# Latent attention on one core: a pair's value products moved into one group in the next even head, its totals moved ahead of the odd head's turn

## The chip, the cores and the metric

The kernel runs on one core of one Trainium2 chip, in one launch. The metric is the device time of that core in microseconds (us); lower is better. All four compute engines take part: TensorE (PE: matmuls, and PEld for the loads of their weights), VectorE (DVE), ScalarE (ACT) and GpSimd (POOL). SyncE (SP) only issues DMAs.

## The reference

Two transformer blocks over 512 tokens of width 1024 are computed one after the other: retention plus sparse attention and a convolution feed-forward, then an mLSTM and gating mixer, two feed-forwards and, between those, the latent attention that the change touches. Cut to that part:

```python
def mla_mixer(h, positions, w_in, q_g, kv_g, w_uq, w_ukv, w_out):
    ...
    qf = jnp.concatenate([q[..., :C_NOPE], q_rope], axis=-1)
    kf = jnp.concatenate([kv[..., :C_NOPE],
                          jnp.broadcast_to(k_rope, (bsz, seq, C_HEADS, C_ROPE))], axis=-1)
    v = kv[..., C_NOPE:]
    scale = (C_NOPE + C_ROPE) ** -0.5
    ...
        s = jnp.einsum("bqhd,bkhd->bhqk", qblk, kf, preferred_element_type=jnp.float32) * scale
        pr = jax.nn.softmax(s, axis=-1)
        return jnp.einsum("bhqk,bkhd->bqhd", pr.astype(v.dtype), v)
    ...
    return o @ w_out
```

There are 16 heads of 64 + 32 query and key columns and 64 value columns, and no mask: every query sees all 512 keys.

## The kernel before, in words

Every engine runs its own list of instructions in the order in which the Python code calls them, and waits on semaphores (`wait_ge`). There is no scheduler: the order on PE is the order of the loop at L1625 to L1656.

The stage works head by head, `n` from 0 to 15, and two heads make a pair, `p = n // 2`. Keys go by four tiles of 128 (`kt`), queries stay 512 wide. Scores and projections split each number into a high and a low part and take three matmuls each (`product`, L771 to L773). For a head PE does:

- `maxima(n)` (L1135): four matmuls of the high parts, from which DVE takes the negated row maxima (`largest_of`, L3088, into `mla_negm`). They are issued one head ahead, into banks 2 and 3 by turns, and wait for DVE to have read their bank (`mx_done`).
- `turn(n)` (L1140): a transpose of the maxima, which DVE spreads into the queries (`shift_of`, L3093, signal `shift_ready`). It waits for all four maxima of head n. `scores(n, 0)` waits for `shift_ready`.
- `scores(n, kt)` (L771 to L773): key by query scores in PSUM bank 4 or 5. ACT takes the exponential (`weights_of`, L1966) into the tile `c_raw` for an even head, `ev` for an odd one. Those tiles are overwritten two heads later, for which ACT waits for the value products (`pv_done`) and for the sums that POOL makes of them (`add_weights`, L733, `weights_added`).
- `values(p, kt)` (L1165): the weights of both heads of pair p times the values of one quarter of the keys, into bank 6 or 7; four calls, each of four matmuls in full float32, which the trace records as eight.
- `totals(p)` (L1178): ones times the POOL sums of both heads, into bank 1. DVE makes reciprocals of them (`shares`, L3100 to L3102), multiplies (`pair_result`, L3109), and ACT and POOL split the result (L1970, L740).
- Projections for coming pairs: `project_nope` and `project_quad` into bank 0, and `project_k` into bank 1.

Bank 1 is thus shared. `project_k(p + 1)`, in even head 2p, leaves the next pair's keys there; ACT takes the high part (L2356) and DVE the low part (`k_lower`, two instructions at L3632, signal `k_low`). `totals(p - 1)`, in odd head 2p + 1, may only overwrite bank 1 when both are done, and says so in L1173: `pe.wait_ge(k_low, min(2 * p + 6, HEADS))`. It waits besides for `weights_added` of its pair and for the earlier totals to be taken.

In an odd head DVE's own order is: the last two maxima of the next head, `k_lower` twice, `shift_of`, the low part of a weight panel (L2433), in every second odd head `quad_take`, then `shares(p - 1)` and `pair_result(p - 1)`.

On PE an odd head n = 2p + 1 ends with `scores(n, 2)`, `turn(n + 1)`, `values(p, 0)`, `values(p, 1)`, `totals(p - 1)`, `scores(n, 3)`, and in heads 1, 5 and 9 a `project_quad`. The even head behind it has `scores(n, 0)`, two maxima, `values(p - 1, 2)`, `values(p - 1, 3)`, `scores(n, 1)`, `project_nope`, two maxima, and so on.

Of the kernel before, what the change touches and what calls it, by code (L numbers as in the profile page):

```python
# [23 lines left out]
NT = S // P  # L24
# [30 lines left out]
PAIRS = HEADS // 2  # L55
# [123 lines left out]
def build_in(nc, A, ctx):  # L179
# [197 lines left out]
    def cols_of(half):  # L377
        return slice(256 * half, 256 * half + 256)
# [68 lines left out]
    def pair_bank(p):  # L447
        return 6 + p % 2

    def weights_tile(n, kt):  # L450
        return (c_raw if n % 2 == 0 else ev)[:, kt, :]

    def weights_sum(n):
        return tmp[:, n % 4, :]
# [313 lines left out]
    def _(pe):  # L768
# [324 lines left out]
        def project_nope(p):  # L1093
            pe.wait_ge(w_lo_ready, pair_panel(p) + 1)
            if p:
                pe.wait_ge(quad_taken, p // 2 + 1)
            if p >= 2:
                pe.wait_ge(nope_low, 2 * p)
            for k in range(3):
                last = product(ps[:, nope_bank(p), :], w(pair_panel(p), k * P, (k + 1) * P), (cq_hi[:, k, :], cq_lo[:, k, :]),  # L1100
                               k == 0, k == 2)
            last.then_inc(nope_done(p)[0], 1)

        def project_k(p, between=None):
            pe.wait_ge(w_lo_ready, pair_panel(p) + 1)
            if p:
                pe.wait_ge(k_low, 2 * p)
            if p >= 3:
                pe.wait_ge(totals_taken, p - 2)
            for k in range(2):  # L1110
                a = 384 + k * P
                if k and between is not None:
                    between()
                last = product(ps[:, 1, :], w(pair_panel(p), a, a + P), (cq_hi[:, 3 + k, :], cq_lo[:, 3 + k, :]), k == 0, k == 1)
            last.then_inc(k_done(p)[0], 1)

        def project_quad(i):
            pe.wait_ge(w_lo_ready, pair_panel(2 * i) + 1)
            if i:
                pe.wait_ge(nope_low, 4 * i)  # L1120
            for k in range(3):
                a = 640 + k * P
                last = product(ps[:, 0, :], w(pair_panel(2 * i), a, a + P), (cq_hi[:, k, :], cq_lo[:, k, :]), k == 0, k == 2)
            last.then_inc(quad_proj, 1)

        def maxima(n, tiles=range(NT)):
            p, slot = n // 2, n % 4
            if tiles.start == 0:
                pe.wait_ge(nope_high, n + 1)
                pe.wait_ge(k_high, n + 1)  # L1130
                pe.wait_ge(rope_placed, 4 * p + 1 + n % 2)
            for t in tiles:
                if 4 * n + t >= 2:
                    pe.wait_ge(mx_done, 4 * n + t - 1)
                nc.tensor.matmul(ps[:, 2 + t % 2, :], q_hi[:, slot, t * P:(t + 1) * P], k_hi[:, slot, :], start=True,  # L1135
                                 stop=True).then_inc(mx_ready, 1)

        def turn(n):
            pe.wait_ge(mx_done, 4 * n + 4)
            nc.tensor.transpose(ps[0:4, 2, 0:P], mla_negm[:, n % 2, :], ident).then_inc(negm_turned, 1)  # L1140

        def scores(n, kt):
            p, slot, m = n // 2, n % 4, 4 * n + kt
            if kt == 0:
                pe.wait_ge(nope_low, n + 1)
                pe.wait_ge(k_low, n + 1)
                pe.wait_ge(rope_placed, 4 * p + 3 + n % 2)
                pe.wait_ge(shift_ready, n + 1)
            if m >= 2:
                pe.wait_ge(exp_done, m - 1)  # L1150
            else:
                pe.wait_ge(v_copied, 7 + m)
            at = slice(kt * P, (kt + 1) * P)
            product(ps[:, 4 + m % 2, :], (k_hi[:, slot, at], k_lo[:, slot, at]), (q_hi[:, slot, :], q_lo[:, slot, :]),
                    True, True).then_inc(s_ready, 1)

        def values(p, kt):

            pe.wait_ge(exp_done, 4 * (2 * p + 1) + kt + 1)
            if kt == 0 and p >= 2:  # L1160
                pe.wait_ge(pair_out, p - 1)
            for half in range(2):
                for a in range(2):
                    n = 2 * p + a
                    last = nc.tensor.matmul(ps[64 * a:64 * a + 64, pair_bank(p), cols_of(half)], mla_v[:, kt, n, :],  # L1165
                                            weights_tile(n, kt)[:, cols_of(half)], start=kt == 0 and half == 0, stop=kt == NT - 1,
                                            skip_group_check=True)
            last.then_inc(pv_done, 1)

        def totals(p):  # L1170

            pe.wait_ge(weights_added, 6 * p + 6)
            pe.wait_ge(k_low, min(2 * p + 6, HEADS))  # L1173
            if p:
                pe.wait_ge(totals_taken, p)
            for half in range(2):
                for a in range(2):
                    last = nc.tensor.matmul(ps[64 * a:64 * a + 64, 1, cols_of(half)], ones[:, 0:64],  # L1178
                                            weights_sum(2 * p + a)[:, cols_of(half)], start=half == 0, stop=True, skip_group_check=True)
            last.then_inc(totals_out, 1)  # L1180
# [444 lines left out]
        for n in range(HEADS):  # L1625
            p, more, even = n // 2, n + 1 < HEADS, n % 2 == 0
            scores(n, 0)
            if more:
                maxima(n + 1, range(0, 2))
            if even and p:  # L1630
                values(p - 1, 2)
                values(p - 1, 3)
            scores(n, 1)
            if even and p + 1 < PAIRS:
                project_nope(p + 1)
            if more:
                maxima(n + 1, range(2, 4))
            scores(n, 2)
            if even:
                if p + 1 < PAIRS:  # L1640
                    project_k(p + 1, between=lambda: turn(n + 1))
                else:
                    turn(n + 1)
                scores(n, 3)
            else:
                if more:
                    turn(n + 1)
                values(p, 0)
                values(p, 1)
                if p:  # L1650
                    totals(p - 1)
                scores(n, 3)
                if n % 4 == 1 and p + 2 < PAIRS:
                    project_quad(p // 2 + 1)
        values(PAIRS - 1, 2)
        values(PAIRS - 1, 3)  # L1656

        def out_part(panel, ks):

# [2278 lines left out]
```

## Time and profile before

| what | us |
|---|---|
| runs of the kernel | 1861.06, 1862.37, 2248.74 |
| their median | 1862.37 |
| the profiled execution, its own time | 1861.49 |
| its span, first to last instruction | 1859.6 |
| PE busy | 1819.3 |
| the stage of latent attention that the change touches, about | 1318 to 1462 of the span |

The rows of the timeline give the start from the span's beginning, the duration, the engine and the line, what is written and read, how often, and in brackets how long the engine was idle before and what released it. Matmuls are pipelined, so durations of neighbours overlap: what a matmul costs is the step from its start to the next start. A place in the stage is found by the turn (L1140), of which there is one a head: the turns of heads 2, 4, 6, 8, 10, 12 and 14, which PE issues in heads 1, 3, 5, 7, 9, 11 and 13, begin at 1334.59, 1353.12, 1370.13, 1389.50, 1406.49, 1425.88 and 1442.88.

### The profile page before, as it was taken

What the parts mean: (1) busy time and instruction counts of PE and PEld (TensorE: products, weight loads), DVE (VectorE), ACT (ScalarE), POOL (GpSimd) and SP (SyncE); (2) the same over time, 40 slices, a digit from 0 to 9 for tenths busy, and PEclk for the clock granted to TensorE, in tenths of its full rate; (3) what the DMA queues carried; (4) which work ended last, traced back from release to release, by engine and by line L of the source; (5) the groups of instructions that cost most, each with busy time, mean ns of one, the idle gap of its engine ahead of it and who ended that gap; (6) DMA issues with size and microseconds to landing.
All of it is one profiled execution on the core that took longest, in us unless ns stands there. A gap on an engine that the chain in (4) does not pass through costs nothing.

```text
span 1859.6 us, 26472 instructions
## 1 busy us (share of the span) xinstructions
PE 1819.3 (98%) x9682; PEld 1505.2 (81%) x9682; DVE 1320.1 (71%) x1805; ACT 814.9 (44%) x1219; POOL 419.6 (23%) x356
## 2 busy tenths in 40 slices
PE   8999999999999999999999999999999999999998
PEld 6787558888888888887888998988666688989897
DVE  7867876784764778777686766786787567758584
ACT  6365334442432444555453434444444344425252
POOL 0021452100000021010034150502477212514230
PEclk9999999999999999999999999999999999999999
DMA  5242013222232332311323232322101123223232
GB/s 217 91 136 69 1 69 102 79 91 101 91 102 91 102 113 80 102 57 46 99 98 104 93 111 92 107 98 79 57 24 34 46 91 102 99 96 112 91 103 91
DMA packets 48239, 166.00 MB, mean 89 GB/s; under 512 B 5376, under 2 KB 7424, under 8 KB 48000
## 3 DMA queue, kind: packets, MB, share of 16 engines
q1 hardware_dynamic: 46512, 161.27, 26.0%
q10 hardware_dynamic: 1616, 3.22, 0.5%
q8 instruction: 73, 1.20, 0.3%
q14 instruction: 38, 0.31, 0.0%
HBM read 162.38 MB, written 2.10 MB: 88 GB/s over the span
## 4 chain that ended last, share of the span: by engine, by line
PE 84%; DVE 10%; ACT 3%; issue 2%; POOL 1%; DMA 0%; SPq 0%; DVEq 0%; ACTq 0%; POOLq 0%
PE ps L771 25%; PE ps L773 24%; PE ps L772 24%; PE ps L1165 2%; DVE w_lo L2433 1%; DVE qk_c L3203 1%; PE ps L1065 1%; POOL x L640 1%; DVE mla_negm L3088 1%; ACT w_hi L1688 1%; DVE tmp L2470 1%; PE ps L993 1%; PE ps L1046 1%; PE ps L1431 1%; PE ps L1135 0%
## 5 line engine op out<-in xcount | busy, mean ns | idle before, releaser
L1688 ACT ACTIVATE w_hi<-raw 128x1024 fp32r<-128x1024 f32 x255 | 269.9, 1058 | 551.5 <-PE ps L773 551.3
L771 PE MATMUL ps<-h_hi,w_hi 128*128 128x512 f32 (+1 forms) x1096 | 412.6, 376 | 8.9 <-DVE w_lo L2714 7.8
L2433 DVE TENSOR_TENSOR w_lo<-raw,w_hi 128x1024 fp32r<-128x1024 f32 x255 | 328.6, 1289 | 109.2 <-ACT w_hi L1688 106.3
L772 PE MATMUL ps<-h_lo,w_hi 128*128 128x512 f32 (+1 forms) x1096 | 403.9, 369 | 0.0
L773 PE MATMUL ps<-h_hi,w_lo 128*128 128x512 f32 (+1 forms) x1096 | 403.8, 368 | 0.0
L771 PE MATMUL ps<-hid_hi,w_hi 128*128 128x512 f32 (+1 forms) x716 | 273.7, 382 | 1.7 <-DVE w_lo L2433 0.9
L772 PE MATMUL ps<-hid_lo,w_hi 128*128 128x512 f32 (+1 forms) x716 | 272.7, 381 | 0.0
L773 PE MATMUL ps<-hid_hi,w_lo 128*128 128x512 f32 (+1 forms) x716 | 272.6, 381 | 0.0
L771 PEld LDWEIGHTS ps<-h_hi,w_hi 128*128 128x128 f32 x1096 | 207.1, 189 | 48.2 <-DVE w_lo L2714 7.8
L773 PEld LDWEIGHTS ps<-h_hi,w_lo 128*128 128x128 f32 x1096 | 207.1, 189 | 34.9
L772 PEld LDWEIGHTS ps<-h_lo,w_hi 128*128 128x128 f32 x1096 | 207.2, 189 | 34.7 <-issue 1.9
L771 PEld LDWEIGHTS ps<-hid_hi,w_hi 128*128 128x128 f32 x716 | 134.6, 188 | 28.7 <-DVE w_lo L2433 2.1
L773 PEld LDWEIGHTS ps<-hid_hi,w_lo 128*128 128x128 f32 x716 | 134.6, 188 | 25.9
L772 PEld LDWEIGHTS ps<-hid_lo,w_hi 128*128 128x128 f32 x716 | 134.6, 188 | 25.6
L2648 DVE TENSOR_TENSOR x<-x,ps 128x512 f32<-128x512 f32 (+1 forms) x82 | 55.2, 673 | 137.9 <-PE ps L773 137.7
L567 POOL TENSOR_TENSOR r<-r,small 128x2 f32<-128x2 f32 x6 | 4.2, 705 | 453.5 <-DVE r L2537 453.5
L673 POOL TENSOR_TENSOR t_f<-raw 128x512 f32<-128x512 f32 x24 | 34.8, 1451 | 279.0 <-DMA raw<-in_panels 270.1
L771 PE MATMUL ps<-s_hi,t_hi 128*128 128x256 f32 x288 | 81.6, 283 | 0.0
L773 PE MATMUL ps<-s_hi,t_lo 128*128 128x256 f32 x288 | 81.5, 283 | 0.0
L772 PE MATMUL ps<-s_lo,t_hi 128*128 128x256 f32 x288 | 81.5, 283 | 0.0
L3402 DVE TENSOR_TENSOR t_lo<-t_f,t_hi 128x1024 fp32r<-128x1024 f32 x48 | 78.9, 1644 | 0.6
L2219 ACT ACTIVATE t_hi<-t_f 128x1024 fp32r<-128x1024 f32 x48 | 49.9, 1053 | 36.1 <-PE ps L773 32.5
(484 smaller groups left out, 3501.9 us busy)
## 6 DMA issues: line engine op xcount, KB each, us to landing
raw<-in_panels SPq DMA_DIRECT2D x295, 512.0 KB, 3.5
x_in<-in_x SPq DMA_DIRECT2D x8, 256.0 KB, 5.9
x<-in_x ACTq DMA_DIRECT2D x1, 2048.0 KB, 9.6
out<-y SPq DMA_DIRECT2D x16, 128.0 KB, 1.8
first<-in_first SPq DMA_DIRECT2D x1, 1568.0 KB, 11.7
raw<-in_panels SPq DMA_DIRECT2D x2, 256.0 KB, 4.9
second<-in_second ACTq DMA_DIRECT2D x1, 512.0 KB, 3.6
small<-in_small ACTq DMA_DIRECT2D x1, 328.0 KB, 4.8
```

The source lines that it names most:

```text
L640: nc.gpsimd.tensor_tensor(x[:, k, at], x[:, k, at], tmp[:, k % 2, at], ALU.add).then_inc(x_ready, 1)
L673: nc.gpsimd.tensor_tensor(out[:, 0, :], right[:, 512:PANEL], right[:, 0:512], ALU.subtract).then_inc(diff_step, 1)
L771: nc.tensor.matmul(out, a[0], b[0], start=start, stop=False)
L772: nc.tensor.matmul(out, a[0], b[1], start=False, stop=False)
L773: return nc.tensor.matmul(out, a[1], b[0], start=False, stop=stop)
L993: nc.tensor.matmul(out, qs[g][:, qt, r["h"] + n, :], rows, start=True, stop=False)
L1165: last = nc.tensor.matmul(ps[64 * a:64 * a + 64, pair_bank(p), cols_of(half)], mla_v[:, kt, n, :], weights_tile(n, kt)[:, cols_of(half)], ...
L1688: nc.scalar.activation(w_high(panel, i), raw[:, panel % 4, :], ACT.Copy).then_inc(w_hi_ready, 1)
L2219: nc.scalar.activation(t_hi[:, at, :], t_f[:, q % 2, at, :], ACT.Copy).then_inc(diff_high, 1)
L2433: signal(V.tensor_tensor(w_low(panel, i), raw[:, panel % 4, :], w_high(panel, i).bitcast(F32), ALU.subtract), w_lo_ready, wait=False)
L2648: signal(V.tensor_tensor(x[:, k, at], x[:, k, at], bank, ALU.add), done)
L3402: signal(V.tensor_tensor(t_lo[:, at, :], t_f[:, q % 2, at, :], t_hi[:, at, :].bitcast(F32), ALU.subtract), diff_low, wait=False)
```

## The change

It edits only the order of calls on PE. The two value calls at the end of the odd head go; the even head behind it makes all four. In the odd head `totals(p - 1)` stands before `turn(n + 1)` where it stood behind the values. Behind the last head all four quarters of the last pair follow each other. The other engines' lists are the same, and so are all waits and all amounts of work.

```diff
             if even and p:
-                values(p - 1, 2)
-                values(p - 1, 3)
+                for kt in range(NT):
+                    values(p - 1, kt)
             scores(n, 1)
...
             else:
+                if p:
+                    totals(p - 1)
                 if more:
                     turn(n + 1)
-                values(p, 0)
-                values(p, 1)
-                if p:
-                    totals(p - 1)
                 scores(n, 3)
                 if n % 4 == 1 and p + 2 < PAIRS:
                     project_quad(p // 2 + 1)
-        values(PAIRS - 1, 2)
-        values(PAIRS - 1, 3)
+        for kt in range(NT):
+            values(PAIRS - 1, kt)
```

On PE, at the end of head 3 (an odd head without `project_quad`), the list before was, from the last value product but one on; L1178 is the totals, the two groups of L771 to L773 behind it are `scores(3, 3)` and `scores(4, 0)`:

```order
L1165 MATMUL ps<-c_raw,mla_v 64x256
L1165 MATMUL ps<-ev,mla_v 64x256
L1178 MATMUL ps<-tmp,small 64x256 x4
L771 MATMUL ps<-q_hi,k_hi 128x512
L772 MATMUL ps<-q_lo,k_hi 128x512
L773 MATMUL ps<-q_hi,k_lo 128x512
```

In the changed kernel the same place reads, from the last matmul of `scores(3, 2)` to the first value products of head 4; L1140 is the turn:

```order
L773 MATMUL ps<-q_hi,k_lo 128x512
L1178 MATMUL ps<-tmp,small 64x256 x4
L1140 MATMUL ps<-small,mla_negm 4x128
L771 MATMUL ps<-q_hi,k_hi 128x512
L772 MATMUL ps<-q_lo,k_hi 128x512
L773 MATMUL ps<-q_hi,k_lo 128x512
L771 MATMUL ps<-q_hi,k_hi 128x512
L772 MATMUL ps<-q_lo,k_hi 128x512
L773 MATMUL ps<-q_hi,k_lo 128x512
L1135 MATMUL ps<-k_hi,q_hi 128x512 x2
L1165 MATMUL ps<-c_raw,mla_v 64x256
L1165 MATMUL ps<-ev,mla_v 64x256
```

The totals now follow the scores of tile 2 directly, the turn stands behind them, and between the turn and `scores(4, 0)` only the three matmuls of `scores(3, 3)` are left.

On DVE nothing moves. Around the same place its list reads, in the numbering of the kernel before:

```order
L3088 TENSOR_REDUCE mla_negm<-ps 128x1 x4
L3632 TENSOR_TENSOR k_lo<-ps,k_hi 64x512 x2
L3093 TENSOR_TENSOR q_hi<-ps,small 4x512
L2433 TENSOR_TENSOR w_lo<-raw,w_hi 128x1024
L3100 STREAM_TRANSPOSE sq<-ps 128x512
```

The maxima (for the turn) stand before the two `k_lower` (for the totals), and `shift_of` behind both.

## Rows read from the trace of the kernel before

**Rows 1.** The profile page: busy time by engine, then the last chain's shares.

```profile
PE 1819.3 (98%) x9682; PEld 1505.2 (81%) x9682; DVE 1320.1 (71%) x1805; ACT 814.9 (44%) x1219; POOL 419.6 (23%) x356
PE 84%; DVE 10%; ACT 3%; issue 2%; POOL 1%; DMA 0%; SPq 0%; DVEq 0%; ACTq 0%; POOLq 0%
```

**Rows 2.** Busy time in the stage: PE, PEld, DVE, ACT, POOL, then clock, DMA.

```profile
1324.00:1462.00 138.00, 134.15 (x708) 89.87 (x707) 101.33 (x151) 65.03 (x109) 94.70 (x84) 1.00 0.11 35
```

**Rows 3.** Timeline of PE, end of head 5.

```profile
1369.42 0.40 PE L773 MATMUL ps<-q_hi,k_lo 128*128 128x512 f32 x1
1370.13 0.27 PE L1140 MATMUL ps<-small,mla_negm 128*4 128x128 f32 x1 [0.31 <-DVE mla_negm L3088]
1370.33 0.43 PE L1165 MATMUL ps<-c_raw,mla_v 128*64 128x256 f32 x1
...
1372.10 1.03 PE L1178 MATMUL ps<-tmp,small 128*64 128x256 f32 x8
1373.07 0.50 PE L771 MATMUL ps<-q_hi,k_hi 128*128 128x512 f32 x1
1373.41 0.39 PE L772 MATMUL ps<-q_lo,k_hi 128*128 128x512 f32 x1
```

**Rows 4.** Timeline of DVE at the same place.

```profile
1368.78 1.29 DVE L3088 TENSOR_REDUCE mla_negm<-ps 128x1 f32<-128x512 f32 x2 [0.22 <-PE ps L1135]
1370.10 1.41 DVE L3632 TENSOR_TENSOR k_lo<-ps,k_hi 64x512 fp32r<-64x512 f32 x2
```

**Rows 5.** Timeline, the same pair of instructions in heads 3 and 13.

```profile
1352.98 1.40 DVE L3632 TENSOR_TENSOR k_lo<-ps,k_hi 64x512 fp32r<-64x512 f32 x2
...
1353.12 0.27 PE L1140 MATMUL ps<-small,mla_negm 128*4 128x128 f32 x1
...
1442.86 1.41 DVE L3632 TENSOR_TENSOR k_lo<-ps,k_hi 64x512 fp32r<-64x512 f32 x2
1442.88 0.27 PE L1140 MATMUL ps<-small,mla_negm 128*4 128x128 f32 x1 [0.32 <-DVE mla_negm L3088]
```

**Rows 6.** Timeline of PE, head 7: tile 3, then tile 0 of head 8.

```profile
1392.44 0.50 PE L771 MATMUL ps<-q_hi,k_hi 128*128 128x512 f32 x1
...
1393.24 0.40 PE L771 MATMUL ps<-q_hi,k_hi 128*128 128x512 f32 x1
```

**Rows 7.** Timeline of PE and DVE, end of head 14.

```profile
1452.33 0.27 PE L1140 MATMUL ps<-small,mla_negm 128*4 128x128 f32 x1 [0.46 <-DVE mla_negm L3088]
...
1452.64 0.68 DVE L3093 TENSOR_TENSOR q_hi<-ps,small 4x512 fp32r<-4x512 f32 x1 [0.36 <-PE ps L1140]
...
1452.91 0.40 PE L773 MATMUL ps<-q_hi,k_lo 128*128 128x512 f32 x1
...
1453.58 0.47 PE L771 MATMUL ps<-q_hi,k_hi 128*128 128x512 f32 x1 [0.27 <-DVE q_hi L3093]
```

**Rows 8.** Timeline of PE, a turn between split products, head 4.

```profile
1364.65 0.27 PE L1140 MATMUL ps<-small,mla_negm 128*4 128x128 f32 x1
1364.68 0.48 PE L771 MATMUL ps<-cq_hi,w_hi 128*128 128x512 f32 x1
1364.99 0.40 PE L772 MATMUL ps<-cq_lo,w_hi 128*128 128x512 f32 x1
```

**Rows 9.** Timeline, slack in head 6: DVE's maxima; PE's maxima, then tile 2.

```profile
1380.02 1.28 DVE L3088 TENSOR_REDUCE mla_negm<-ps 128x1 f32<-128x512 f32 x2
...
1381.88 0.62 PE L1135 MATMUL ps<-k_hi,q_hi 128*128 128x512 f32 x2
1382.33 0.39 PE L771 MATMUL ps<-q_hi,k_hi 128*128 128x512 f32 x1
```

**Rows 10.** Timeline of PE, the first matmuls of the kernel.

```profile
8.41 0.63 PE L772 MATMUL ps<-h_lo,w_hi 128*128 128x512 f32 x1
8.83 0.63 PE L773 MATMUL ps<-h_hi,w_lo 128*128 128x512 f32 x1
...
11.37 0.40 PE L773 MATMUL ps<-h_hi,w_lo 128*128 128x512 f32 x1
```

## The prediction

> **What bounds the kernel now.** I read the page first. PE is busy 1819.3 us of a span of 1859.6, and 84% of the chain that ended last is PE [rows 1]. Next comes the stretch of the stage: from 1324 to 1462 PE is busy 134.15 of 138.00 us, with DVE at 101, POOL at 95 and ACT at 65 us, and the granted clock reads 1.00, the 2.4 GHz level [rows 2]. So PE sets the time here as elsewhere, and a change of order on PE can act in two ways only: PE idles longer or less, or its matmuls follow each other in steps that are longer or shorter. The amount of work is the same. I therefore went to the timeline of PE at the places that are reordered, and beside it to that of DVE, since the waits of the moved calls (the totals for `k_low`, the turn for `mx_done`, the scores for `shift_ready`) are all on DVE.
>
> In head 5 PE starts its last matmul of `scores(5, 2)` at 1369.42 and is done by 1369.82. It idles 0.31 us and turns at 1370.13 [rows 3]. DVE ended the maxima at 1368.78 + 1.29 = 1370.07, so the turn starts 0.06 us after its releaser. DVE then goes on to `k_lower`, 1370.10 to 1371.51 [rows 4]. The totals, which need `k_low`, come at 1372.10 [rows 3], 0.6 us after it. What keeps PE busy between 1370.33 and 1372.10 is the two value calls. They are the cover of the `k_low` wait, and the change takes them away.
>
> **Term A: the totals wait for `k_low`.** The totals now follow `scores(n, 2)`, and PE starts them only when `k_lower` ends. Measured from the start of the old turn, that is 1371.51 - 1370.13 = 1.38 us in head 5 [rows 3, 4], 1352.98 + 1.40 - 1353.12 = 1.26 in head 3 and 1442.86 + 1.41 - 1442.88 = 1.39 in head 13 [rows 5]. Heads 7 and 11 read as head 3 and head 9 as head 5, to 0.01. Six heads do this, 3 to 13: head 1 has no totals, and in head 15 no new keys are projected. The sum is 3 x 1.26 + 3 x 1.39 = 7.9 us, plus the 0.06 of a handover each, 0.4: **+8.3 us**. That is beyond the old wait for the maxima, since I count from the turn's old start. `k_lower` itself can't come sooner: it is behind the same maxima on DVE, whose matmuls PE issues before `scores(n, 2)` in both versions. The other waits of the totals have been met long before: the sums of pair p - 1 are those of heads two and three back.
>
> Behind the waiting totals stand the turn, `scores(n, 3)` and the whole of the next head. The turn and tile 3 have what they need 1.4 us earlier, but stand in the same queue. On this hangs the term. The Trainium skill, in TensorE: Matmul & The Clock Gate, section The mechanism of Part 3, says that matmuls keep program order in start and end and that only weight loads are pulled ahead. By that rule the term stands in full, 8.3 us; if later matmuls could pass the waiting totals it would be near nothing. The trace agrees as far as it goes: no row here shows a matmul passing another.
>
> **Term B: `scores(n + 1, 0)` waits for the shift.** Before, values and totals lay between the turn and `scores(n, 3)`, 2.94 us [rows 3]. Now the turn is directly before it, and in heads without `project_quad` `scores(n + 1, 0)` follows 0.80 us later [rows 6]. The trace has exactly this sequence once, at the end of head 14: turn at 1452.33, three matmuls, then `scores(15, 0)`, which could start at 1452.91 + 0.23 = 1453.14 but starts at 1453.58, after DVE's 0.68 us shift and its signal [rows 7]. That is 0.44 us, in heads 3, 7, 11 and 13: **+1.8 us**. In heads 5 and 9 (and 1) the projection, 9 matmuls of 0.23, covers it.
>
> **Term C: steps between kinds of matmul.** A change of kind costs a little. In the old order of head 5 it takes 0.20 from the turn to the first value product, and after the totals (8 x 0.107 = 0.86 of 0.97 us) 0.11, with the first split matmul at a step of 0.34 where 0.23 is usual: 0.11 more [rows 3]. With 0.05 for a long first step of the values that is 0.47 us. In the new order the totals start out of an idle (0.05), the turn behind them is taken at 0.10 (an estimate: one matmul of the totals' kind), and a turn with the split products behind it costs 0.03 + (0.31 - 0.23) = 0.11 [rows 8], in all 0.26. So 0.2 us is saved in each of six heads, 1.2. In head 1, which has values but no totals, 0.47 becomes 0.11: 0.4 us. The value products cost 0.107 us each in either place; the group of the even head grows from 1.7 to 3.4 us and needs no further change of kind. **-1.6 us**, between 0 and -2.5.
>
> **What moves at no cost.** The even head's group now starts with quarters 0 and 1. `exp` of tile 0 of that head must wait for quarter 0 (its tile is overwritten), some 1.4 us later (two maxima 0.5, a quarter 0.9) against PE's `scores(n, 0)` than before. The next PE call that needs it is `scores(n, 2)`, behind all four quarters (3.4 us) and nine matmuls of a projection (2.1 us): over 3 us of cover. DVE gets its turn 1.2 us later in the odd head; its next deadline is the first two maxima in the even head, which it had done at 1380.02 + 1.28 = 1381.30, and PE asked at 1381.88 [rows 9]. PE asks later too, by the new wait less the saved steps, 1.2 us, so the slack of 0.6 stays. If it were gone, the rest would be paid per head (a rival below). The tail: before, values, totals, tile 3, values; after, totals, tile 3, values. The last exponential is needed by quarter 3, which has 2.6 us of value products ahead of it. I take 0, within +-0.3. No DMA and no queue of SP or POOL is touched.
>
> **Sum.** 8.3 + 1.8 - 1.6 = +8.5 us on the profiled execution's own 1861.49 (1859.6 of span and 1.9 around it): 1870.0 us, or 0.5% slower. The median of the shown runs is 0.9 above the profiled one, so 1871 would be as good; I keep the profiled base. Ends of the unknowns: A from 7.5 to 8.5, B from 0 (the signal arrives in the shadow of the steps that C saves) to 2.4, C from -2.5 to 0. That gives 1866.5 to 1872.4, and 1 us more by the base.
>
> **Rivals.** *Not slower.* The values' removal between turn and tile 3 brings tile 3 and its exponential forward, and only the saved steps remain: 1861.5 - 1.6 = 1860 us. The place is the start of the totals; it decides if `k_lower` ends by the time `scores(n, 2)` does, 1369.8 in head 5. For it: the totals waited for nothing before. Against it: `k_lower` ended at 1371.51 [rows 4], and in all six heads it began 0.02 to 0.14 before the turn. Chance 0.07.
>
> *A knock-on.* The turn comes 1.2 us later on DVE's clock, its panel, shares and pair result follow, and the maxima of the even head aren't ready when PE asks; each of six heads loses up to 1.2 us more, 7.2 in all: 1877 us. For it: DVE had only 0.6 us of slack there [rows 9]. Against: PE asks later too. Chance 0.08.
>
> *The clock.* PE now idles from 1369.82 to 1371.57, 1.75 us, every pair, where the idles in the rows shown were 0.31 to 0.46 [rows 3, 5, 7]. After the 7.8 us of idle at the start, seven steps took 0.42 where 0.23 follows, from 8.41 to 11.37 [rows 10]: 1.4 us lost. Once in each of six heads: 8.4 more, 1878 us. Against: the stretch reads 1.00 with all its idle. Chance 0.03. The Trainium skill, in TensorE: Matmul & The Clock Gate, section HAM oscillation, says that repeated idle stretches take the clock to half again and again; by it this rival is what to look for, and no row of this stage shows it.
>
> **How the numbers follow.** My forecast has 0.82, not slower 0.07, the knock-on 0.08, the clock 0.03. The range of 8 in 10 is the forecast's own with a little to both sides, 1865 to 1874 us; it leaves out the far rivals. A measurement of this kernel tells about 2% from no change, 37 us. No case reaches that: within 2% gets 0.97, faster 0.01, slower 0.02.
>
> **What would show it.** In the changed profile the first of the totals' matmuls in heads 3 to 13 has an idle of about 1.7 us before it, released by `k_lo` of L3630, 8.3 us more than the 0.9 or so that the turns there waited; the turn's own wait is gone. `scores(n + 1, 0)` shows 0.3 to 0.4 us released by the shift in four heads. The stage lasts 8.5 us longer, and every other stage is as long as before. The forecast is wrong if the stage is no longer than before, if the totals start without an idle, or if an idle appears before the maxima or the value group of the even head.

## The result and the profile after

The changed kernel takes 1872.8 us in the median of six runs (1870.42 to 1875.35), against 1862.14 before. The ratio is 1.0054, with a 95% interval from 1.0044 to 1.0064: slower by half a percent, and by about 10 us. One of the six runs before took 2248.74 us; the ratio leaves it out. The forecast was 1870.0 us, with a range of 1865 to 1874. The profiled execution took 1873.01 us, 11.5 more than that of before.

The page of the changed kernel reads nearly as [rows 1]: PE is busy 3 us longer, in a span that is 11.6 us longer.

```profile
PE 1822.3 (97%) x9682; PEld 1507.3 (81%) x9682; DVE 1320.2 (71%) x1805; ACT 815.4 (44%) x1219; POOL 422.4 (23%) x356
PE 83%; DVE 9%; ACT 3%; issue 2%; POOL 2%; DMA 0%; DVEq 0%; ACTq 0%; SPq 0%; POOLq 0%
```

The same instructions with 3 us more of PE time is the first sign of something beside waiting. The list of who waited for whom, of the changed kernel from 1315 to 1490 (engine, line, releaser, then us in total, times, longest), shows the rest:

```profile
PE ps L1178 <- POOL tmp L733: 5.4, 3, 1.8
PE ps L1178 <- issue: 2.9, 2, 1.4
PE ps L771 <- DVE q_hi L3091: 2.1, 5, 1.0
PE ps L1178 <- DVE k_lo L3630: 1.5, 1, 1.5
PE ps L1140 <- DVE mla_negm L3086: 0.5, 1, 0.5
```

Three rows belong to the totals (L1178): 6 waits, 9.8 us. Before, the totals had no such row, and the turn waited 0.31 in three heads besides the 0.46 of head 14 [rows 3, 5, 7]; the latter alone is left. The shift behind the turn (L3091) is waited for five times, 2.1 us in all, where it was twice and 1.3 before: that is term B. Three of these waits are new, in heads 3, 7 and 11, each 0.28 us of idle; the fourth that was forecast, in head 13, doesn't show in this execution, since the clock fell there (below). The three rows of the totals name three releasers for one wait. Which it was is told by the timelines of head 5. That of PE answers to [rows 3]:

```profile
1370.58 0.40 PE L773 MATMUL ps<-q_hi,k_lo 128*128 128x512 f32 x1
1372.77 1.08 PE L1178 MATMUL ps<-tmp,small 128*64 128x256 f32 x8 [1.79 <-POOL tmp L733]
1373.78 0.27 PE L1140 MATMUL ps<-small,mla_negm 128*4 128x128 f32 x1
1373.81 0.48 PE L771 MATMUL ps<-q_hi,k_hi 128*128 128x512 f32 x1
1374.13 0.39 PE L772 MATMUL ps<-q_lo,k_hi 128*128 128x512 f32 x1
```

That of DVE in the same head answers to [rows 4]:

```profile
1371.26 1.41 DVE L3630 TENSOR_TENSOR k_lo<-ps,k_hi 64x512 fp32r<-64x512 f32 x2
1374.09 0.68 DVE L3091 TENSOR_TENSOR q_hi<-ps,small 4x512 fp32r<-4x512 f32 x1 [1.42 <-PE ps L1140]
```

`k_lower` ends at 1372.67 and the totals start 0.10 later. The POOL sum that is named is of a later head: POOL's last sum of the pair whose totals these are was ready at 1360.27, 12 us before. In all six heads the totals start 0.10 to 0.14 after the end of `k_lower`. The idle before them is 1.8 us in heads 5, 9 and 13, and 1.4 to 1.5 in heads 3, 7 and 11, where the turn had not waited before. DVE for its part now idles 1.42 us until the turn.

What the forecast gave only 0.03 happened as well, in part. The same place in head 9 of the same execution:

```profile
1409.90 0.40 PE L773 MATMUL ps<-q_hi,k_lo 128*128 128x512 f32 x1
1412.10 1.70 PE L1178 MATMUL ps<-tmp,small 128*64 128x256 f32 x8 [1.80 <-POOL tmp L733]
1413.73 0.37 PE L1140 MATMUL ps<-small,mla_negm 128*4 128x128 f32 x1
1413.76 0.78 PE L771 MATMUL ps<-q_hi,k_hi 128*128 128x512 f32 x1
1414.33 0.63 PE L772 MATMUL ps<-q_lo,k_hi 128*128 128x512 f32 x1
1414.76 0.63 PE L773 MATMUL ps<-q_hi,k_lo 128*128 128x512 f32 x1
```

The totals take 1.63 us to the turn where head 5 has 1.01, and the steps between split matmuls are 0.43 where 0.23 is usual, up to 1415.96. The view by windows of the changed kernel (PE, PEld, DVE, ACT, POOL busy, then the granted clock, the DMA share and GB/s) shows the granted clock down, around head 9 and then around head 13, and whole around head 3 for comparison:

```profile
1352.00:1356.00 4.00, 2.41 (x14) 1.07 (x13) 2.47 (x5) 0.64 (x2) 3.76 (x4) 1.00 0.00 0
1411.00:1414.00 3.00, 1.90 (x10) 1.01 (x11) 0.97 (x2) 0.00 (x0) 1.61 (x2) 0.74 0.00 0
1453.00:1456.00 3.00, 2.95 (x12) 1.57 (x13) 0.89 (x2) 0.00 (x0) 0.63 (x1) 0.56 0.00 0
```

In those stretches PE ran in part at its lower level, 1.2 GHz. The Trainium skill, in TensorE: Matmul & The Clock Gate, section HAM oscillation, says that repeated gaps of waiting take the clock to half. The trace agrees that it happens, here with gaps of 1.8 us, which are shorter than those of the page's example, and at two of the six gaps only.

**A measure that is free of the rest of the kernel.** The granted clock also falls now and then far from the stage: windows of 20 us read 0.91 at 680 in the profile of before and 0.92 at 300 in that of after, and each 1.00 at the other's place. So times of whole runs vary by 1 to 3 us for reasons that are not the change's. I therefore compare the distance from the turn of head 1 to that of head 15, the second and the last L1140 of the stage. In the changed kernel these are

```profile
1328.01 0.27 PE L1140 MATMUL ps<-small,mla_negm 128*4 128x128 f32 x1
...
1463.88 0.27 PE L1140 MATMUL ps<-small,mla_negm 128*4 128x128 f32 x1 [0.46 <-DVE mla_negm L3086]
```

a distance of 135.87 us. Before it was 1452.33 [rows 7] less 1328.24, 124.09. That is +11.8 us, all of the 11.5 by which the executions differ and the 0.3 that other places gave back.

### The profile page after: what moved, and what is told of

The parts are those of the page before. It is cut to its first block, busy times and chain, and to the rows that moved or that the text cites. A ratio compares the mean times of both kernels' runs of the same rounds, so it can differ in the third digit from the quotient of the medians.

```text
span 1871.2 us, 26472 instructions
## 1 busy us (share of the span) xinstructions
PE 1822.3 (97%) x9682; PEld 1507.3 (81%) x9682; DVE 1320.2 (71%) x1805; ACT 815.4 (44%) x1219; POOL 422.4 (23%) x356
## 4 chain that ended last, share of the span: by engine, by line
PE 83%; DVE 9%; ACT 3%; issue 2%; POOL 2%; DMA 0%; DVEq 0%; ACTq 0%; SPq 0%; POOLq 0%
PE ps L771 25%; PE ps L772 24%; PE ps L773 24%; PE ps L1165 2%; DVE w_lo L2431 1%; PE ps L1065 1%; DVE qk_c L3201 1%; POOL x L640 1%; ACT w_hi L1686 1%; DVE tmp L2468 1%; PE ps L993 1%; PE ps L1046 1%; PE ps L1178 1%; PE ps L1431 0%; PE ps L962 0%
## 5 line engine op out<-in xcount | busy, mean ns | idle before, releaser
L771 PE MATMUL ps<-h_hi,w_hi 128*128 128x512 f32 (+1 forms) x1096 | 412.8, 377 | 8.3 <-DVE w_lo L2712 7.9
L773 PE MATMUL ps<-h_hi,w_lo 128*128 128x512 f32 (+1 forms) x1096 | 404.1, 369 | 0.0
L771 PE MATMUL ps<-hid_hi,w_hi 128*128 128x512 f32 (+1 forms) x716 | 273.7, 382 | 1.7 <-DVE w_lo L2431 0.9
L773 PE MATMUL ps<-hid_hi,w_lo 128*128 128x512 f32 (+1 forms) x716 | 272.6, 381 | 0.0
L771 PEld LDWEIGHTS ps<-h_hi,w_hi 128*128 128x128 f32 x1096 | 207.2, 189 | 47.8 <-DVE w_lo L2712 7.9
L773 PEld LDWEIGHTS ps<-h_hi,w_lo 128*128 128x128 f32 x1096 | 207.2, 189 | 35.0
L771 PEld LDWEIGHTS ps<-hid_hi,w_hi 128*128 128x128 f32 x716 | 134.6, 188 | 28.9 <-DVE w_lo L2431 2.1
L773 PEld LDWEIGHTS ps<-hid_hi,w_lo 128*128 128x128 f32 x716 | 134.6, 188 | 25.8
L771 PE MATMUL ps<-s_hi,t_hi 128*128 128x256 f32 x288 | 81.7, 284 | 0.0
L773 PE MATMUL ps<-s_hi,t_lo 128*128 128x256 f32 x288 | 81.5, 283 | 0.0
## 6 DMA issues: line engine op xcount, KB each, us to landing
first<-in_first SPq DMA_DIRECT2D x1, 1568.0 KB, 11.5
```

The costliest lines, as they stand in the source:

```text
L771: nc.tensor.matmul(out, a[0], b[0], start=start, stop=False)
L773: return nc.tensor.matmul(out, a[1], b[0], start=False, stop=stop)
```

## The experiments

Ten more runs were made, of seven new kernels, two of them twice, and once more of the changed one. The table gives for each run the distance between those two turns less the 124.09 of before, the granted clock's falls in the stage, and the time over all runs; the median of before beside them was 1861.7 to 1862.2 us each time.

| kernel | turn to turn | falls | median us | ratio to before, interval |
|---|---|---|---|---|
| changed | +11.8 | 2 | 1872.80 | 1.0054, 1.0044 to 1.0064 |
| changed_again | +10.2 | 1 | 1872.43 | 1.0056, 1.0042 to 1.0069 |
| filled_wait | +9.2 | 0 | 1871.15 | 1.0048, 1.0031 to 1.0065 |
| filled_again | +9.2 | 0 | 1871.48 | 1.0048, 1.0035 to 1.0062 |
| totals_only | +9.5 | 0 | 1872.86 | 1.0062, 1.0046 to 1.0077 |
| turn_first | +7.1 | 0 | 1870.22 | 1.0042, 1.0026 to 1.0059 |
| totals_behind_tile3 | +3.0 | 0 | 1864.65 | 1.0014, 1.0004 to 1.0023 |
| longer_wait | +18.5 | 4 | 1880.85 | 1.0099, 1.0084 to 1.0115 |
| other_bank | -0.0 | 0 | 1862.45 | 1.0000, 0.9991 to 1.0010 |
| other_bank_nope_early | -2.1 | 0 | 1860.90 | 0.9993, 0.9984 to 1.0002 |
| nope_early_again | -2.2 | 0 | 1859.78 | 0.9991, 0.9982 to 1.0000 |

**Which half of the change costs?** The first half-change moves only the totals.

```diff
             else:
+                if p:
+                    totals(p - 1)
                 if more:
                     turn(n + 1)
                 values(p, 0)
                 values(p, 1)
-                if p:
-                    totals(p - 1)
                 scores(n, 3)
```

> The kernel before with the second half of the change alone: the totals stand ahead of the turn in the odd head, the values stay where they were, two quarters behind the turn. Theory: the wait for k_low is all there (+8.3 us), the shift is covered by the values (no term B), and the steps between kinds save nothing or 0.2 us a head: 1869 us, and up to 1873 if the clock falls in two heads. Rival (it is the move of the values that costs): within 1.5 us of the kernel before.

It costs 9.5 us from turn to turn, without any fall of the clock in the stage. The rival, that the move of the values costs, is out. The median, 1872.86, is nearly 4 us above the 1869 that was expected without falls: of the 10.7 us by which its profiled execution is over that of before, 1.2 lie outside the stage (the granted clock reads 0.91 from 1520 to 1540, where before it read 1.00), and what the other runs spent isn't known. The profile of totals_only at head 5 has the same wait:

```profile
1372.77 1.08 PE L1178 MATMUL ps<-tmp,small 128*64 128x256 f32 x8 [1.80 <-POOL tmp L733]
```

So the wait for `k_low` came with the totals' new place, wherever the values stand. With the values in the even head alone and the totals behind the turn or behind tile 3, it shrinks by what PE does meanwhile:

```diff
-                if p:
-                    totals(p - 1)
                 if more:
                     turn(n + 1)
+                if p:
+                    totals(p - 1)
                 scores(n, 3)
```

> The changed kernel with turn and totals exchanged in the odd head: scores, turn, totals, tile 3. Theory: the totals wait for k_low still (+8.3), but the shift runs on VectorE during their time, so term B (1.8) vanishes; PE's idle is cut in two by the turn and is about 1.2 instead of 1.5 to 1.8 us, so the clock falls more seldom or not. 1868 to 1869.5 us. Rival (the turn behind the waiting totals is what costs, the queue behind them being late): 1863 us or less.

The profile of turn_first at head 5:

```profile
1371.67 0.27 PE L1140 MATMUL ps<-small,mla_negm 128*4 128x128 f32 x1 [0.30 <-DVE mla_negm L3086]
1373.16 1.08 PE L1178 MATMUL ps<-tmp,small 128*64 128x256 f32 x8 [1.21 <-POOL tmp L733]
```

+7.1 us. That is 2.1 below the filled kernels (further down), where I had said 1.8 for term B; the wait for the shift is gone from its list but for heads 0 and 14, which had it before. The totals still begin 1.49 after the turn. So what stands behind the totals in the queue costs the 2 us of term B, and the totals' own wait the larger rest. The time, 1870.2, is 0.7 above what I had expected at most.

```diff
-                if p:
-                    totals(p - 1)
                 if more:
                     turn(n + 1)
                 scores(n, 3)
+                if p:
+                    totals(p - 1)
```

> The changed kernel with the totals behind tile 3 of the odd head: scores, turn, tile 3, totals. Theory: tile 3 (0.8 us) now covers part of the k_low wait, 0.6 us of it is left in each of six heads (+3.6), no wait for the shift, steps between kinds as before the change save in head 1 (-0.4), no fall of the clock: 1865 us. Rival (the waits cost little and the grouped values a lot): 1870 us or more.

The profile of totals_behind_tile3 at head 5:

```profile
1371.32 0.27 PE L1140 MATMUL ps<-small,mla_negm 128*4 128x128 f32 x1 [0.32 <-DVE mla_negm L3086]
...
1372.81 1.08 PE L1178 MATMUL ps<-tmp,small 128*64 128x256 f32 x8 [0.51 <-issue]
```

Again the totals begin 1.49 us after the turn, since `k_lower` sets that and not PE. But tile 3 lies between, and PE idles 0.51 instead of 1.79. +3.0 us from turn to turn, 1864.65 in the median: as expected.

**Does the wait vanish with its cause?** Since the values of pair p are now all in the even head, the pair bank that they will fill is free in the odd head. The totals of pairs 0 to 5 go there, bank 1 is left to the keys, and the wait for `k_low` has no reason any more. DVE takes the totals directly behind the shift, so that the bank is free again in time.

```diff
+    def total_bank(p):
+        return pair_bank(p + 1) if p < PAIRS - 2 else 1
...
+            if kt == 0 and 1 <= p < PAIRS - 1:
+                pe.wait_ge(totals_taken, p)
...
-            pe.wait_ge(k_low, min(2 * p + 6, HEADS))
+            if p >= PAIRS - 2:
+                pe.wait_ge(k_low, HEADS)
+            elif p:
+                pe.wait_ge(pair_out, p)
...
                     shift_of(n + 1)
+                if 1 <= p < PAIRS - 1:
+                    take_totals(p - 1)
```

> The changed kernel, with the totals of pairs 0 to 5 in the pair bank that is free in the odd head, so that they no longer wait for k_low; VectorE reads them directly behind the shift. PE's order is that of the changed kernel. Theory: term A (8.3 us) and the falls of the clock (3 us) vanish; the saved steps (-1.6) stay; the totals fill what PE idled before the turn (about -1.4); the wait for the shift in heads 3, 7, 11 and 13 is 0.6 us each, since the shift now stands behind k_lower while PE is early (+2.4). In all 1861 us, within 1 us of the kernel before. Rival (it is the grouping of the values, or the later exponentials, that costs): 1868 us or more, with idles of PE in the even heads.

The timeline of PE in other_bank at the end of head 7 (L1186 are the totals, L1143 is the turn, L774 begins a split product):

```profile
1388.53 0.40 PE L776 MATMUL ps<-q_hi,k_lo 128*128 128x512 f32 x1
1388.86 1.08 PE L1186 MATMUL ps<-tmp,small 128*64 128x256 f32 x8
1389.87 0.27 PE L1143 MATMUL ps<-small,mla_negm 128*4 128x128 f32 x1
...
1390.45 0.40 PE L776 MATMUL ps<-q_hi,k_lo 128*128 128x512 f32 x1
1391.25 0.47 PE L774 MATMUL ps<-q_hi,k_hi 128*128 128x512 f32 x1 [0.40 <-DVE q_hi L3099]
```

No idle before the totals, no fall of the clock, and 0.57 us (1391.25 less 1390.45 + 0.23) for the shift, where 0.6 was expected. In head 13 it is 1.00 us, from 1443.68 + 0.23 to 1444.91; DVE ends its shift 0.34 us later behind the turn there than in head 7. The distance is that of before to 0.03 us, and the ratio 1.0000. The order of the change is thus not bad in itself: with bank 1 free its net cost is nothing. Term A is gone; the waits for the shift are still there, and the saved steps and the turn's old waits, which the totals now fill, pay for them. DVE's list differs from that of the changed kernel too (it takes the totals earlier), so this is not a change of the bank alone.

**The clock.** Six more matmuls per pair, whose result nobody reads, fill most of PE's idle. Their one wait, for the pair bank, held PE up nowhere:

```diff
+        def filler(p):
+
+            if p >= 2:
+                pe.wait_ge(pair_out, p - 1)
+            for _ in range(6):
+                nc.tensor.matmul(ps[:, pair_bank(p), :], cq_hi[:, 0, 0:P], cq_hi[:, 0, :], start=True, stop=True)
...
+                if 1 <= p < PAIRS - 1:
+                    filler(p)
                 if p:
                     totals(p - 1)
```

> The changed kernel, with six extra matmuls (128x512, high parts only, results never read) ahead of the totals in heads 3 to 13, written into the pair bank that is free there. They add no wait and fill 6 x 0.23 = 1.4 us of the 1.5 to 2.0 us that PE idles there. Theory (the idle for k_low costs its own length, and on top of it now and then lets the granted clock fall, 1.6 us each time, in two heads of the profiled run): the totals start when they did, the granted clock stays at 1.00 all through the stage, the totals never take 1.7 us, and the time is 3 us below the changed kernel, 1869 to 1870 us. Rival (the 3 us over the sum of my three terms come from somewhere else, such as the grouped values or other waits): 1873 us as before, or 8 us more if the idle was not really there.

In the profile of filled_wait the totals stand where they stood, and the last turn comes 2.6 us earlier against the first:

```profile
1370.66 0.39 PE L773 MATMUL ps<-q_hi,k_lo 128*128 128x512 f32 x1
1370.88 1.53 PE L1175 MATMUL ps<-cq_hi 128*128 128x512 f32 x6
1372.84 1.08 PE L1185 MATMUL ps<-tmp,small 128*64 128x256 f32 x8 [0.42 <-issue]
```

PE does 36 matmuls more and the stage is shorter. The time is 1871.15 us, 1.6 below the changed kernel, though not the 3 that I expected: my sum of the three terms was too low by 0.7, and the first profile had shown two falls where others have one or none. The two kernels were then run side by side.

> The changed kernel as it is, a second time, beside filled_again on the same chip. Theory (each pair's idle of 1.5 to 1.8 us may or may not let the clock fall, depending on when it comes): its profile again has falls of the granted clock inside the stage, at one to three of the waits of heads 5, 9 and 13, not necessarily the same ones; its times lie 1 to 3 us over filled_again and spread wider. Rival (the two falls of the first profile were a chance of that one execution): none in the stage, and the same time as filled_again within 0.5 us.

> filled_wait a second time. Theory: the stage is at 1.00 throughout, 9.2 us longer than in the kernel before from the turn of head 1 to that of head 15, 1871 us. Rival as for changed_again.

The second profile of the changed kernel has one fall, in head 13, and +10.2 us; the filled one none and +9.2, as the first time. In the times the difference is 1 us in the medians (1872.43 and 1871.48). Over both comparisons the filled kernel is lower by 1.0 and by 1.6 us, but the intervals of their ratios overlap; that the falls cost about 1 us of the median is likely, not shown by the times alone. What the profiles show is that the stage has falls only in kernels with an idle of 1.8 us or more in it, though not in each of them (totals_only has none).

The counterpart makes the idle longer. DVE does the first `k_lower` of each pair twice.

```diff
             dve.wait_ge(k_high, n + 1)
+            if n >= 4 and n % 2 == 0:
+                link(V.tensor_tensor(k_lo[r, n % 4, :], ps[r, 1, :], k_hi[r, n % 4, :].bitcast(F32), ALU.subtract))
```

> The changed kernel with one more VectorE instruction of 0.7 us (the first k_lower of each pair, done twice) ahead of the k_low signal in heads 3 to 13. Theory: PE's idle before the totals grows by 0.7 us in six heads, +4.3 us, and with 2.2 to 2.7 us of idle the granted clock falls in more of the heads than in two, up to all six, 1.6 us each and more: 1880 us, between 1877 and 1885. Rival (falls of the clock have nothing to do with the length of this idle): +4.3 alone, 1877 us, with two slow heads.

The windows of longer_wait behind the totals of heads 3, 5, 7 and 9, then of heads 11 and 13:

```profile
1355.00:1361.00 6.00, 5.36 (x25) 3.13 (x27) 3.47 (x5) 0.60 (x1) 4.80 (x4) 0.72 0.01 1
1376.00:1382.00 6.00, 5.82 (x24) 4.13 (x25) 2.41 (x5) 0.60 (x1) 1.39 (x2) 0.75 0.07 13
1398.00:1404.00 6.00, 5.24 (x23) 3.30 (x25) 4.20 (x5) 0.60 (x1) 5.52 (x5) 0.72 0.01 3
1419.00:1425.00 6.00, 5.63 (x22) 4.05 (x23) 2.18 (x3) 0.60 (x1) 1.52 (x2) 0.72 0.14 29
1442.00:1448.00 6.00, 5.52 (x38) 3.42 (x40) 4.44 (x8) 1.32 (x3) 5.72 (x4) 1.00 0.20 66
1461.00:1467.00 6.00, 4.88 (x33) 3.00 (x35) 4.44 (x7) 1.00 (x2) 2.25 (x2) 1.00 0.10 21
```

Four falls with idles of 2.2 to 2.5 us. The stage is 9.3 us longer than the filled one: 6 x 0.72 = 4.3 of idle and 5.0 for four falls, 1.25 each. The changed kernel gives (11.8 - 9.2) / 2 = 1.3 each, and its second profile 10.2 - 9.2 = 1.0 for its one. Head by head (an odd head's turn to that of the next odd head, less the same in filled_wait, and less 0.72 in longer_wait) a fall costs 1.0 to 1.1 us in heads 3, 7 and 13, and 1.3 to 1.6 in heads 5 and 9. In the former the wait for the shift is missing from the trace: the slow steps lie over it. The rival (no more falls than before, 1877 us) is out; 1880.85 is near the 1880 that was expected.

**A version that keeps the saved steps.** It is other_bank with one thing more. In heads 4, 8 and 12 `project_nope`, which needs nothing that is late, is put between tile 3 and `scores(n, 0)`, where the shift was waited for.

```diff
+            early = n % 4 == 0 and n and p + 1 < PAIRS
+            if early:
+                project_nope(p + 1)
             scores(n, 0)
...
-            if even and p + 1 < PAIRS:
+            if even and p + 1 < PAIRS and not early:
                 project_nope(p + 1)
```

> As other_bank, and in heads 4, 8 and 12 the projection project_nope stands ahead of the first scores, so that it covers the wait for the shift behind heads 3, 7 and 11. Theory: three of the four waits of 0.6 us go: 1.7 us below other_bank, about 1859.5 us, 0.1% faster than the kernel before. Rival: the exponentials of the even head come 2 us later for it and something else waits: no gain over other_bank.

> other_bank_nope_early a second time, since its first comparison, 0.9993 of the kernel before, had an interval that touches 1. Theory: 2.1 us less from the turn of head 1 to that of head 15, as in its first profile, and 0.9989 of the kernel before, 1860 us. Rival: the gain is given back outside the stage, ratio 1.000.

Both profiles are 2.1 to 2.2 us shorter from turn to turn than before, and both comparisons lie below 1, 0.9993 and 0.9991, with intervals that end at 1.0002 and 1.0000. It is the fastest of all kernels here, by 1 to 2 us or 0.1% over the kernel before, at the edge of what so many runs can tell.

## Why the prediction was right

*Term A, the wait of the totals for `k_low`,* +8.3 us: right in place and mechanism, and in size but for 0.3 us. The totals began 1.49 us after the turn where a turn precedes them (turn_first, totals_behind_tile3), or 1.36 to 1.41 in heads 3, 7 and 11, against the 1.45 and 1.32 of the working: the handover took 0.10 to 0.15 where I had taken the 0.06 of the turn. That adds 0.3 us in six heads. The idle of "about 1.7 us" that was to show it is right for heads 5, 9 and 13; in the other three it is 1.4 to 1.5. The wait went when its bank went (other_bank).

*Term B, the shift,* +1.8 us: right in mechanism, a little too small. The changed kernel's timeline at the end of head 7 repeats [rows 7] to 0.01 us, 1.24 from the turn to `scores(8, 0)`:

```profile
1394.33 0.27 PE L1140 MATMUL ps<-small,mla_negm 128*4 128x128 f32 x1
...
1394.90 0.40 PE L773 MATMUL ps<-q_hi,k_lo 128*128 128x512 f32 x1
1395.57 0.47 PE L771 MATMUL ps<-q_hi,k_hi 128*128 128x512 f32 x1 [0.28 <-DVE q_hi L3091]
1395.88 0.39 PE L772 MATMUL ps<-q_lo,k_hi 128*128 128x512 f32 x1
```

The working left out that the first matmul behind such a wait takes a step of 0.31 us (1395.57 to 1395.88) where 0.23 is usual: 0.3 us more in four heads, or 2.1 in all, which is about what turn_first saved. In both profiles of the filled kernel all four waits are there, of 0.28 us and once 0.37.

*Term C, the steps saved,* -1.6 us: right where it can be read apart. From the turn of head 1 (issued at the end of head 0) to that of head 3 there is no totals call and no new wait; 1347.31 - 1328.24 = 19.07 before and 1346.72 - 1328.01 = 18.71 after, 0.36 less, as worked out for head 1 (0.47 less 0.11). The totals in front of the turn take 1.01 and the turn 0.03 and a long step, as forecast. For the other heads the term isn't measured by itself.

Head by head, the filled kernel's turns are later than before by 1.7 to 1.8 us for each odd head without a projection behind it, where the terms gave 1.6 to 1.7, and by 1.3 with one, where they gave 1.2 to 1.3. The sum without clock is +9.2 where 8.5 was forecast; of the 0.7, the handover is 0.3 and the long step behind the shift 0.3.

*What moves at no cost* stayed so: beside those for the shift no wait appeared in the even heads or at the tail (from the last turn to the last totals it is 10.88 us before and 10.87 after), and PE shows no idle before the value group.

*The rivals.* "Not slower" is out by the ratio's interval, and by its own test: `k_lower` ended 1.7 us after `scores(5, 2)` did (1372.67, and 1370.58 + 0.40). "A knock-on" didn't occur; the maxima of the even head were never waited for anew. "The clock" got 0.03, and this is where the prediction fell short. The argument against it was that the stretch read 1.00 with all its idle; but that idle was 0.3 to 0.6 us at a time, and the new one is 1.4 to 1.8, a length of which the stage had no example. It was also taken as all or nothing. It happened at one or two of six waits and cost 1.0 to 1.6 us each, which puts the profiled time at 1873 instead of 1871. My price of 1.4 us each, from the first matmuls of the kernel [rows 10], was good. That the time lies in the range is thus in part luck: the median is 10.7 us over that of before, near the 10.9 that the upper ends of the three terms add up to, while the terms themselves came to 9.2. The room left for them covered a cause that had been all but ruled out.

## What to carry to other kernels

Before a call is moved ahead on a full engine, look at what its waits had for cover: here 1.8 us of value products hid a wait that no view of the profile listed, since it had never been waited for. The number to read is not a wait but the distance between the end of the releasing instruction and the start of the waiting one. And if two uses of one buffer are what the wait is for, see whether the new order has left another buffer free; here that gave back the whole 9.2 us.

## What the runs showed of the hardware

Behind an idle of TensorE of 1.8 us the granted clock fell to its lower level at some of the places where it occurs (of heads 5, 9 and 13, at 9 and 13 in one execution, at 13 alone in another, at none in totals_only), and behind one of 2.2 to 2.5 us at four of six. The idles of 1.4 to 1.5 us in heads 3, 7 and 11 of the same three executions had no fall, and neither had idles of 0.4 to 1.2 us in the stage (filled_wait, turn_first, totals_behind_tile3). That does not make these lengths safe: outside the stage, in the profile of before, the clock reads 0.50 from 691 to 694, behind two idles of 0.79 us that follow each other closely:

```profile
688.62 0.61 PE L855 MATMUL ps<-small,sq 128*128 128x1 f32 x4 [0.79 <-ACT sq L1750]
690.02 0.36 PE L771 MATMUL ps<-h_hi,w_third 128*128 128x256 f32 x1 [0.79 <-DVE h_lo L2565]
...
691.00:694.00 3.00, 3.00 (x14) 2.96 (x14) 3.00 (x7) 1.63 (x4) 2.25 (x4) 0.50 0.00 0
```

What decides at which idle the clock falls is open. A fall cost 1.0 to 1.6 us, and 36 matmuls of no use, put into the idle, made the stage shorter, by 2.6 and by 1.0 us.

The handover from a VectorE instruction to a waiting matmul took 0.05 to 0.06 us for the turn, 0.10 to 0.15 for the totals and 0.26 for the scores behind the shift; why they differ is open. The releaser that the profile names for the totals' wait, which is on three semaphores, changed from head to head, POOL, issue or DVE. The true one was `k_lower` each time: the totals start 0.10 to 0.15 us behind its end in every head, and they start 0.7 later behind the scores where it is made 0.7 longer (longer_wait).
